# Streaming the experts' weights of a 32-expert mixture in 2 MB transfers with 16 KB runs per partition, through a ring of eight slots instead of sixteen

## The reference

```
logits = xf @ router_w + router_b
top_val, top_idx = top_k(logits, 4);  gates = softmax(top_val)
for each expert e, over the tokens that chose it:
    hid  = xb @ moe_w1[e] + moe_b1[e]            # w1[e] is 1024 x 2048
    gate = min(hid[:, :1024], 7);  lin = clip(hid[:, 1024:], -7, 7)
    act  = gate * sigmoid(1.702 * gate) * (lin + 1)
    out  = act @ moe_w2[e] + moe_b2[e]           # w2[e] is 1024 x 1024
y[token] += gates[token, e] * out
```

## Time and profile before

| | before |
|---|---|
| median of 3 executions | 1168.07 us |
| the profiled execution's own time | 1168.59 us |
| its span, first to last instruction | 1166.70 us |
| TensorE busy / mean granted clock | 94% / 0.981 |
| VectorE, ScalarE, GpSimd busy | 29%, 14%, 6% |
| transfers of expert weights | 384 of 1 MB, 22.2 us from issue to landing (median) |
| bytes moved, mean over the span | 425.75 MB (millions of bytes), 365 GB/s |

### The profile page before, as it was taken

One profiled execution on the slowest core, in us unless ns is written; L12 is line 12 of the kernel. 1 busy time (PEld: TensorE's weight loads), 2 busy tenths in 40 slices (PEclk: granted clock), 3 DMA queues, 4 the chain that ended last, 5 costly groups with the idle time before them and its releaser, 6 DMA issues.

```text
span 1166.7 us, 14398 instructions
## 1 busy us (share of the span) xinstructions
PE 1096.3 (94%) x5399; PEld 463.8 (40%) x5399; DVE 340.8 (29%) x798; ACT 166.2 (14%) x290; POOL 72.9 (6%) x119
## 2 busy tenths in 40 slices
PE   6999898999999999999999999999999999999994
PEld 3666546433333343434343333333333333333331
DVE  3489855212121212121212121212121212121215
ACT  3444122100111010001000100010100100010002
POOL 8501440000000000000000000000000000000000
PEclk9999797999999999999999999999999999999998
DMA  9431645799999999999999999999999999999991
GB/s 311 160 145 73 260 177 197 284 397 417 417 418 418 418 418 418 418 418 418 417 417 418 417 418 417 418 418 417 417 418 417 418 417 418 418 417 418 417 417 65
DMA packets 84734, 425.75 MB, mean 365 GB/s; under 512 B 10145, under 2 KB 14374, under 8 KB 51937
## 3 DMA queue, kind: packets, MB, share of 16 engines
q1 hardware_dynamic: 82793, 423.69, 89.7%
q0 software_dynamic: 1920, 1.80, 0.6%
HBM read 423.50 MB, written 2.17 MB: 365 GB/s over the span
## 4 chain that ended last, share of the span: by engine, by line
SPq 45%; PE 41%; DVE 5%; DMA 5%; issue 3%; ACT 1%; ACTq 0%; DVEq 0%
SPq L470 44%; PE bank L1654 14%; PE bank L1309 8%; PE bank L1689 7%; DMA ring<-in_moe_w_dram 4%; PE bank L1604 3%; PE bank L1619 2%; PE bank L1344 1%; PE bank L1560 1%; DVE ring L996 1%; PE bank L1525 1%; SPq L469 1%; PE bank L1669 1%; PE bank L1390 0%; PE bank L1314 0%
## 5 line engine op out<-in xcount | busy, mean ns | idle before, releaser
L1654 PE MATMUL bank<-ring,hT 128*64 128x512 f32 x2048 | 464.8, 597 | 33.1 <-DMA ring<-in_moe_w_dram 31.7
L1654 PEld LDWEIGHTS bank<-ring,hT 128*64 128x64 f32 x2048 | 138.2, 136 | 341.7 <-issue 228.9
L1689 PE MATMUL bank<-ring 128*64 128x512 f32 x1024 | 230.3, 597 | 0.0
L1263 DVE TENSOR_SCALAR ring<-bank 128x512 f32<-128x512 f32 x32 | 22.1, 692 | 395.6 <-PE bank L1654 395.6
L1689 PEld LDWEIGHTS bank<-ring 128*64 128x64 f32 x1024 | 69.3, 137 | 146.6 <-issue 140.1
L1604 PEld LDWEIGHTS bank<-ring,xt 128*128 128x128 f32 x792 | 93.3, 196 | 27.9 <-issue 26.0
L1604 PE MATMUL bank<-ring,xt 128*128 128x128 f32 x792 | 99.6, 283 | 1.8 <-DVE ring L1195 1.8
L1201 DVE COPY hT<-bank 128x512 f32<-128x512 f32 x33 | 22.6, 684 | 255.5 <-PE bank L1604 255.5
L837 ACT ACTIVATE ring<-ring 128x512 f32<-128x512 f32 x32 | 20.2, 630 | 512.5 <-DVE ring L1263 512.5
L846 ACT ACTIVATE ring<-bank 64x512 f32<-64x512 f32 x64 | 37.8, 591 | 243.9 <-PE bank L1689 243.1
L1212 DVE TENSOR_TENSOR ring<-ring,bank 128x512 f32<-128x512 f32 x68 | 43.4, 676 | 87.3 <-PE bank L1619 87.2
(11 more groups left out here) (290 smaller groups left out, 614.1 us busy)
## 6 DMA issues: line engine op xcount, KB each, us to landing
ring<-in_moe_w_dram SPq DMA_DIRECT2D x384, 1024.0 KB, 22.2
ring<-in_w_out_dram SPq DMA_DIRECT2D x2, 2048.0 KB, 9.4
ring<-in_w_in_dram SPq DMA_DIRECT2D x2, 1536.0 KB, 17.4
ring<-in_w_in_dram SPq DMA_DIRECT2D x1, 3072.0 KB, 24.6
ring<-in_w_in_dram SPq DMA_DIRECT2D x1, 2048.0 KB, 13.5
ring<-in_w_in_dram SPq DMA_DIRECT2D x1, 1600.0 KB, 8.7
lnbc<-in_ln_g_dram SPq DMA_DIRECT2D x3, 512.0 KB, 15.9
lnbc<-in_ln_b_dram SPq DMA_DIRECT2D x3, 512.0 KB, 11.1
```

Source lines behind the costliest of these rows:

```text
L1654: ins = pe.matmul(bank[b][64 * h:64 * h + 64, :], xT[:, q, k, j * CAP:(j + 1) * CAP], ring[:, c:c + 512], start=False, stop=k == KT - 1)
L1689: ins = pe.matmul(bank[4][64 * h:64 * h + 64, :], a, ring[:, c:c + 512], start=k == 0, stop=k == KT - 1)
```

## The change

An expert is now six pieces of 2 MB, four of w1 and two of w2, and the ring has eight slots of 4096 floats per partition: the same 16 MB. A piece of w1 is 256 rows, of which partition p holds rows 2 p and 2 p + 1, 16 KB that follow each other in memory. A piece of w2 is 512 rows, of which partition p holds rows 4 p to 4 p + 3, also 16 KB in one run. Each partition's rows are other rows of the product than before, so the stationary operands follow: `gather` reads every second column of `xt`, and the transpose of the activation reads every fourth column of `l1`. `w_used` goes up once in two k-steps of w1 and once in four of w2. The mixer's own places in `ring` stay where they were (MB1 = 2048).

```diff
-PIECES = 12
-SLOTS = 16
+PIECES = 6
+W1P = 4
+SLOTS = 8
 GROUP = 4
-SLOT = 2048
+SLOT = 4096
+MB1 = 2048
...
         def w1_piece(e, s):
-            return moe_w1[0, bass.ds(e, 1), s * P:(s + 1) * P, :].rearrange("a p c -> p (a c)")
+            return moe_w1[0, bass.ds(e, 1), s * 2 * P:(s + 1) * 2 * P, :].rearrange("a (p t) c -> p (a t c)", t=2)
 
         def w2_piece(e, s):
-            r = (s - 8) * 2 * P
-            return moe_w2[0, bass.ds(e, 1), r:r + 2 * P, :].rearrange("a (t p) c -> p (a t) c", p=P)
+            r = (s - W1P) * 4 * P
+            return moe_w2[0, bass.ds(e, 1), r:r + 4 * P, :].rearrange("a (p t) c -> p (a t c)", t=4)
...
-            for s in w1_order[0:6]:
+            for s in w1_order[0:3]:
                 load_first(s)
             sp.wait_ge(ya_ready, MA)
             sp.wait_ge(outcols_ready, 2)
             sp.dma_start(wout[:, 4:8, :], w_out[0, 4 * P:8 * P, :].rearrange("(k p) n -> p k n", p=P)).then_inc(ld_wout[1], 16)
-            for s in w1_order[6:8]:
+            for s in w1_order[3:4]:
                 load_first(s)
...
                 for k in range(4 * half, 4 * half + 4):
                     out = bank[(2, 5)[k // 4]][:, (k % 4) * 2 * CAP:(k % 4 + 1) * 2 * CAP]
+                    c = 2 * P * (k // 2) + k % 2
                     for t in range(3):
-                        ins = pe.matmul(out, xt[:, t, k * P:(k + 1) * P], pick[:, t, :], start=t == 0, stop=t == 2)
+                        ins = pe.matmul(out, xt[:, t, c:2 * P * (k // 2 + 1):2], pick[:, t, :], start=t == 0, stop=t == 2)
...
-                                at_ = slot_of(k)
+                                if k % 2 == 0:
+                                    at_ = slot_of(k // 2)
                                 for b in range(2):
                                     for h in range(2):
-                                        c = at_ + (2 * b + h) * 512
+                                        c = at_ + k % 2 * MB1 + (2 * b + h) * 512
                                         ins = pe.matmul(bank[b][64 * h:64 * h + 64, :], xT[:, q, k, j * CAP:(j + 1) * CAP],
                                                         ring[:, c:c + 512], start=False, stop=k == KT - 1)
-                                ins.then_inc(w_used, 1)
+                                if k % 2 == 1:
+                                    ins.then_inc(w_used, 1)
...
-                                ins = pe.transpose(bank[3][:, k * P:(k + 1) * P], l1[:, k * P:(k + 1) * P], ident[:, :])
+                                ins = pe.transpose(bank[3][:, k * P:(k + 1) * P], l1[:, k:512:4], ident[:, :])
...
-                                if k % 2 == 0:
-                                    at_ = slot_of(8 + k // 2)
+                                if k % 4 == 0:
+                                    at_ = slot_of(W1P + k // 4)
...
-                                if k % 2 == 1:
+                                if k % 4 == 3:
                                     ins.then_inc(w_used, 1)
```

More of the change, by code:

```diff
@@ L143, in build_kernel @@
         valid = sb("valid", [P, 3])
-        top = {"mixer": PIECES * SLOT, "moe": SLOTS * SLOT}
+        top = {"mixer": 12 * MB1, "moe": SLOTS * SLOT}
         def part(phase, *shape):
@@ L226, in in_ring @@
             at[0] += n
-            assert at[0] <= PIECES * SLOT
+            assert at[0] <= 12 * MB1
             v = ring[:, a:a + n]
@@ L248, in build_kernel @@
             off += KT * n
-        assert off <= 10 * SLOT
+        assert off <= 10 * MB1
         def freed_by(a, b):
             return max((job for x, y, job in spans if x < b and a < y), key=J.get)
-        wout = ring[:, 8 * SLOT:12 * SLOT].rearrange("p (k n) -> p k n", n=D)
+        wout = ring[:, 8 * MB1:12 * MB1].rearrange("p (k n) -> p k n", n=D)
         p2 = ring[:, vm_at:vm_at + D]
@@ L368, in w1_piece, with slot @@
         def w1_piece(e, s):
-            return moe_w1[0, bass.ds(e, 1), s * P:(s + 1) * P, :].rearrange("a p c -> p (a c)")
+            return moe_w1[0, bass.ds(e, 1), s * 2 * P:(s + 1) * 2 * P, :].rearrange("a (p t) c -> p (a t c)", t=2)
         def w2_piece(e, s):
-            r = (s - 8) * 2 * P
-            return moe_w2[0, bass.ds(e, 1), r:r + 2 * P, :].rearrange("a (t p) c -> p (a t) c", p=P)
+            r = (s - W1P) * 4 * P
+            return moe_w2[0, bass.ds(e, 1), r:r + 4 * P, :].rearrange("a (p t) c -> p (a t c)", t=4)
+        def slot(s):
+            return ring[:, s * SLOT:(s + 1) * SLOT]
         @block.sync
@@ L407, in _ @@
             sp.dma_start(rb[:, :], router_b.to_broadcast([P, NE])).then_inc(ld_router, 16)
-            filled(sp, freed_by(8 * SLOT, 10 * SLOT))
+            filled(sp, freed_by(8 * MB1, 10 * MB1))
             sp.dma_start(wout[:, 0:4, :], w_out[0, 0:4 * P, :].rearrange("(k p) n -> p k n", p=P)).then_inc(ld_wout[0], 16)
-            w1_order = sorted(range(8), key=lambda s: J[freed_by(s * SLOT, (s + 1) * SLOT)])
+            w1_order = sorted(range(W1P), key=lambda s: J[freed_by(s * SLOT, (s + 1) * SLOT)])
             def load_first(s):
                 filled(sp, freed_by(s * SLOT, (s + 1) * SLOT))
-                sp.dma_start(ring[:, s * SLOT:(s + 1) * SLOT], moe_w1[0, 0, s * P:(s + 1) * P, :]).then_inc(w_full[s], 16)
-            for s in w1_order[0:6]:
+                sp.dma_start(slot(s), moe_w1[0, 0, s * 2 * P:(s + 1) * 2 * P, :].rearrange("(p t) c -> p (t c)", t=2)
+                             ).then_inc(w_full[s], 16)
+            for s in w1_order[0:3]:
                 load_first(s)
@@ L433, in _ @@
             for s in range(PIECES, SLOTS):
-                sp.dma_start(ring[:, s * SLOT:(s + 1) * SLOT], moe_w1[0, 1, (s - PIECES) * P:(s - PIECES + 1) * P, :]
+                r = (s - PIECES) * 2 * P
+                sp.dma_start(slot(s), moe_w1[0, 1, r:r + 2 * P, :].rearrange("(p t) c -> p (t c)", t=2)
                              ).then_inc(w_full[s], 16)
@@ L441, in _ @@
             filled(sp, "P11")
-            for s in range(8, PIECES):
-                sp.dma_start(ring[:, s * SLOT:(s + 1) * SLOT].rearrange("p (t c) -> p t c", t=2),
-                             moe_w2[0, 0, (s - 8) * 2 * P:(s - 7) * 2 * P, :].rearrange("(t p) c -> p t c", p=P)
+            for s in range(W1P, PIECES):
+                r = (s - W1P) * 4 * P
+                sp.dma_start(slot(s), moe_w2[0, 0, r:r + 4 * P, :].rearrange("(p t) c -> p (t c)", t=4)
                              ).then_inc(w_full[s], 16)
@@ L464, in load_group @@
                         s = k % SLOTS
[L465 to L468, removed]
+                        src = w1_piece(ei, c) if c < W1P else w2_piece(ei, c)
+                        dst = slot(s)
                         sp.wait_ge(w_used, PIECES * n + k - SLOTS + 1)
@@ L1260, in _ @@
                             n, e = 2 * pi + j, GROUP * g + 2 * q + j
-                            dve.wait_ge(w_used, PIECES * n + KT)
+                            dve.wait_ge(w_used, PIECES * n + W1P)
                             dve.tensor_scalar(g1[:, :], bank[0][:, :], LIMIT, None, ALU.min).then_inc(g1_ready, 1)
```

4 lines of the change are left out of this document (2 added, 2 removed).

## The result

The changed kernel takes 1150.28 us (median of four executions, 1150.01 to 1152.18). The kernel before took 1167.2 us beside it, so the ratio is 0.9854, 95% interval 0.9841 to 0.9866: 17 us faster. The forecast was 1147 us in a range of 1140 to 1172. In the runs further down, two executions at a lower granted clock (1192.99 us at 0.917 and 1623.56 us at 0.649, where all others have about 0.98) stand in no ratio, and as the second was the profiled one of the kernel that changes w1 only, no row of that kernel is read.

What follows compares the result with a forecast made beforehand. The arrival of weights, the queue of transfers, was taken as the bound. Stream -24.7, first release +1.7, starving 0, tail +1.7 sum to -21.3 us against 1168.59: 1147.3, stated as 1147 us, range 1140 to 1172.

Steps and rivals of the forecast that it cites:

- B and o: In the weight stream, an engine's time for its bytes of a 1 MB piece (2.403 us) and per packet (0.010 us).
- The first rival: Weight stream: only w2's 4 KB runs were slow, so only w2 gains, 9.9 us; 1162 us, chance 0.13.
- The second: Weight stream: no faster, coarser ring adds 3.4 us, 1172 us; 1191 us if runs are cut to 4 KB; chance 0.13.
- The third: Gathers on TensorE: strided loads take twice as long, TensorE becomes the bound, a pair takes 61.4 us; 1214 us, chance 0.06.
- the gain of the stream: 368 MB of weights streamed after the mixer's loads: runs of 16 KB take 899.0 us instead of 923.7, -24.7 us.
- The first release: Start of the mixture: SyncE's first issue waits for `w_used`, which comes a k-step later, +1.7 us.
- The tail: After the last piece of w1 lands, TensorE has two k-steps left instead of one, +1.7 us.
- Starving at the start: Early mixture: with few slots freed the stream runs dry; extra cost taken as 0, 3 us to either side.
- The mixer: Before the mixture: `wout`'s second half lands 4.9 us later, at 135.6, but is used at 145.09; zero cost.

Runs made afterwards that it cites:

- the first experiment: The change's 2 MB pieces and eight slots, but with the runs and column order of the kernel before; 1172.6 us, ratio 1.0053.
- The gather's move: The changed kernel with its second gather ahead of the fifth k-step instead of the fourth; 1149.82 us, ratio 0.9847.

## Why the prediction was right

**The bound and its reading.** The queue of transfers set the end before and sets it after. (Its 417 to 418 GB/s begin in the tenth slice, not the ninth, which reads 397.) The split of an expert's 30.12 us into 2.483 us for each MB of w1 and 2.563 us for w2 was right, and so was the model of bytes and packets made from it. The line through 4 and 8 KB, B = 2.403 and o = 0.010 us, gave 4.886 us for 2 MB in runs of 16 KB, and 4.89 was measured. The experiments follow it over a factor of eight in the run. The last columns are the packets that an engine moves in one pair of experts (24 MB), the length of a pair once TensorE waits for transfers, and that length by B and o:

| runs | rate, 400 to 1000 us, GB/s | by B and o | packets | a pair, us | by B and o |
|---|---|---|---|---|---|
| 4 KB | 410 | 409 | 384 | 61.44 | 61.51 |
| 4 KB in w2, 8 KB in w1 | 418 | 418 | 256 | 60.25 | 60.23 |
| 8 KB | 422 | 422 | 192 | 59.65 | 59.59 |
| 16 KB | 428 to 429 | 429 | 96 | 58.73 | 58.63 |
| 16 KB in w2, 32 KB in w1 | 430 | 432 | 64 | 58.43 | 58.31 |

The lengths are read between two starts of the second layer, seven pairs apart (ten for 4 KB). In the order of the table (for 8 KB, the kernel before with w2's runs lengthened), with one row for each of the two kernels whose later row is shown above, 1078.65 and 1061.68:

```profile
485.87 7.09 PE L1707 MATMUL bank<-ring 128*64 128x512 f32 x32
1100.27 7.09 PE L1707 MATMUL bank<-ring 128*64 128x512 f32 x32
656.89 7.09 PE L1689 MATMUL bank<-ring 128*64 128x512 f32 x32
649.46 7.09 PE L1687 MATMUL bank<-ring 128*64 128x512 f32 x32
1067.04 7.09 PE L1687 MATMUL bank<-ring 128*64 128x512 f32 x32
650.57 7.09 PE L1697 MATMUL bank<-ring 128*64 128x512 f32 x32
712.94 7.09 PE L1695 MATMUL bank<-ring 128*64 128x512 f32 x32
1121.94 7.09 PE L1695 MATMUL bank<-ring 128*64 128x512 f32 x32
```

All five lie within 0.02 us of one line, 57.83 us and 9.4 ns for a packet. So one price per packet holds from 4 to 32 KB, and it is a little less than the 10 ns that two near numbers had given.

**The first rival** (only w2 gains) falls with the experiment that changes w1 alone. The Trainium skill (DMA: Bandwidth & Descriptors, on why small descriptors are slow) has some 3 cycles per packet, an estimate of 3.5 ns at its 850 MHz; these runs do not bear it out, they need 9.4 ns. **The second** falls with the packets of 16 KB and the rate of 428. **The third** did not happen in the change, though its price was right. With a stride of four floats the gather doubles, a pair takes 61.25 us (61.4 in the prediction) and the kernel 1213 us (1214). The Trainium skill's rule on cachelines (SBUF - State Buffer) fits the gather: with two floats to a 16-byte line 0.14 us more for 24 loads, with one float twice the time. For the four transposed blocks it does not show: strides of two and of four both show medians of 208 and 209 ns a load, and the chain has 0.47 to 0.57 us for the four in the change, against 0.44 to 0.63 us before.

**The size that was off** is the gain of the stream, put at 24.7 us. Against the profiled execution the forecast was 1147.3 and 1150.0 was measured, 2.7 us more: 0.4 us is a longer mixer, and the mixture's stretch gained 18.9 us instead of 21.3. The first release cost 1.72 us, as forecast. The tail cost 1.8: 34.7 us from the last wait to the end before (1166.7 - 1132.02), 36.5 after (1148.2 - 1111.73). From the first issue to the last wait for a transfer the gain is (1132.02 - 210.54) - (1111.73 - 212.69) = 22.4 us where the term had 24.7. The 2.3 us have three parts.

- The price of a packet. A pair gains 60.25 - 58.73 = 1.52 us where the forecast had 1.60, so a packet costs 9.5 ns between these two kernels and not 10. Over the 368 / 24 = 15.3 pairs of the stream that is 1.2 us.
- The count. The 24.7 us count all 368 MB, but the last wait is for the last piece of w1. The 4 MB of w2 behind it gain 4 x 2.563 - 2 x 4.886 = 0.5 us, and nothing waits for them.
- Starving at the start, put at 0 with 3 us to either side. What is left for it is 0.6 us.

The stretches from the first issue to 260 us, before and after, say the same in kind:

```profile
210.54:260.00 49.46, 49.46 (x257) 20.11 (x255) 12.07 (x29) 4.13 (x7) 0.00 (x0) 1.00 0.97 381
212.69:260.00 47.31, 47.31 (x245) 19.77 (x243) 12.07 (x29) 4.13 (x7) 0.00 (x0) 1.00 0.95 379
```

At 418 and 428 GB/s the same bytes would have taken 4.4 and 5.4 us less, so the start loses some 1 us more than it did, a little more than the 0.6. But it is not a fixed price of coarser slots. In the first experiment, with the old runs in the same slots, the first issue and the last wait are

```profile
212.22 26.72 SPq L476 DMA_DIRECT2D ring<-in_moe_w_dram  x6
...
1132.66 3.65 PE L1662 MATMUL bank<-ring,hT 128*64 128x512 f32 x16 [1.33 <-DMA ring<-in_moe_w_dram]
```

which is 920.4 us against 921.5 before, 1 us less. Why it is less there and more in the change is not settled. The gather's move shows that a gap at the start can shift without its cost going away.

**The mixer** was put at zero, and its one term came true: the second half of `wout` was forecast at 135.6 us. It was issued at 119.53 us, landed 16.8 us later, at 136.3, and was needed at 145.45:

```profile
119.53 0.38 SPq L428 DMA_DIRECT2D ring<-in_w_out_dram  x1
DMA to landing us min/median/max: 16.8/16.8/16.8
145.45 9.18 PE L1530 MATMUL bank<-ring 128*64 128x512 f32 x32
```

The start of the mixture differs by 1.3 us between two profiles of the changed kernel, so an effect of some tenths on the mixer could not be seen.

## What to carry to other kernels

When a stream of transfers is the bound, compare the time per byte of transfers with different runs in the same trace: two lengths give a line in packets and bytes, and the line prices a longer run before it is built. Lengthen the run, not the transfer, and stop where the coarser slots cost as much at the two ends as the packets save; between 16 and 32 KB nothing was left here. When the longer run reorders the rows, look at the operand that has to follow it: a stride of two floats in TensorE's stationary operand cost 0.14 us for a gather of 24 loads, hidden in TensorE's spare time, and a stride of four doubled the gather's time and cost 62 us.

## What the runs showed that I had not expected

The length that a strided load shows says little: 208 ns for a transposed block with a stride of two floats, 209 with four, against 141 plain, but 197 in the gather with a stride of two (192 plain) and 330 with four (medians). Only the length of 24 loads in a row (2.88, 3.02 and 5.80 us) told the cost.

Transfers to 64 partitions, every other one, in turn with transfers to the other 64, fill the ring as fast as transfers to all 128: 429 GB/s. One such transfer by itself was not measured.
